# The high half of the transposed activations: a second activation from PSUM on ACT in place of a cast on DVE

## What is computed

```
h   = rmsnorm(x, g_norm1)   * (1 + sc1) + sh1          # 512 x 1024
hc  = rmsnorm(ctx, g_norm1) * (1 + mods_c1) + mods_c0  # 256 x 1024
P   = h @ w_in ; pc = hc @ w_in[:, :1312]              # split among three token mixers and the gates
x   = x + gt1 * (merge of the three mixers) @ w_out
h2  = rmsnorm(x, g_norm2) * (1 + sc2) + sh2            # 512 x 1024
x   = x + gt2 * ((silu(a) * b) @ w_ffn_out),  a, b = split(h2 @ w_ffn_in)
out = rmsnorm(x, g_final)
```

## Time and profile before

| | |
|---|---|
| median of three runs | 1573.95 us (1573.01 to 1574.51) |
| the profiled execution | 1574.66 us, of which 1572.8 us is the span from its first to its last instruction |
| PE busy | 1279.3 us, 81% of the span |
| DVE busy | 644.2 us, 41% |
| ACT busy | 369.8 us, 24% |
| POOL busy | 355.7 us, 23% |
| mean granted clock of PE | 0.864 of full speed |

### The profile page before, as it was taken

The page is one execution under the profiler, slowest core; times in us unless marked ns, Lnnn a source line. Parts: engine busy times, 40 slices in busy tenths (PEclk is TensorE's granted clock), DMA queues, the critical chain, the costliest instruction groups (busy, mean ns, idle before and its releaser), DMA issues.

```text
span 1572.8 us, 14451 instructions
## 1 busy us (share of the span) xinstructions
PE 1279.3 (81%) x5761; PEld 944.0 (60%) x5761; DVE 644.2 (41%) x1007; ACT 369.8 (24%) x458; POOL 355.7 (23%) x148
## 2 busy tenths in 40 slices
PE   5579998476966778787669787898967999999994
PEld 1246877355744556665555434665946888888883
DVE  3445225234274766766731858333432000310023
ACT  2364212031212222222104000021042222123212
POOL 2002124002021202102104011030313454455541
PEclk9988989555788887878759898999968999999998
DMA  9320224611011202112114021335351332333211
GB/s 331 106 94 27 81 78 117 103 54 54 27 59 62 60 7 74 34 37 83 35 19 175 25 82 40 113 101 187 100 142 54 88 100 94 104 84 108 83 65 54
DMA packets 137712, 131.45 MB, mean 84 GB/s; under 512 B 12986, under 2 KB 125818, under 8 KB 136621
## 3 DMA queue, kind: packets, MB, share of 16 engines
q1 hardware_dynamic: 115936, 99.81, 20.9%
q10 hardware_dynamic: 17292, 13.22, 3.7%
q0 software_dynamic: 4416, 17.50, 3.1%
HBM read 119.49 MB, written 8.91 MB: 82 GB/s over the span
## 4 chain that ended last, share of the span: by engine, by line
PE 51%; DVE 17%; issue 3%; ACT 2%; ACTq 1%; DMA 1%; POOL 1%; DVEq 0%; POOLq 0%
PE psum L640 43%; DVE buf L2008 2%; DVE buf L2007 2%; PE psum L856 1%; DVE buf L1851 1%; DVE buf L1849 1%; PE psum L838 1%; PE psum L847 1%; PE psum L794 1%; ACTq L1374 1%; PE psum L790 1%; DVE buf L2004 1%; DVE buf L1834 1%; DVE buf L1832 1%; DVE buf L1833 1%
## 5 line engine op out<-in xcount | busy, mean ns | idle before, releaser
L1115 POOL TENSOR_TENSOR ring_lo<-buf,ring_hi 128x2048 fp32r<-128x2048 f32 (+1 forms) x65 | 293.5, 4516 | 891.7 <-ACT ring_hi L1265 891.7
L640 PE MATMUL psum<-hT_hi,ring_hi 128*128 128x512 f32 x744 | 312.9, 421 | 16.9 <-DVE hT_lo L2074 10.0
L640 PE MATMUL psum<-hT_lo,ring_hi 128*128 128x512 f32 x744 | 298.6, 401 | 0.0
L640 PE MATMUL psum<-hT_hi,ring_lo 128*128 128x512 f32 x744 | 297.8, 400 | 0.0
L640 PE MATMUL psum<-buf,buf 128*128 128x512 f32 (+1 forms) x480 | 215.5, 604 | 61.8 <-DVEq L1534 15.6
L640 PEld LDWEIGHTS psum<-buf,buf 128*128 128x128 f32 x480 | 97.5, 206 | 166.3 <-issue 112.2
L1265 ACT ACTIVATE ring_hi<-buf 128x2048 fp32r<-128x2048 f32 (+1 forms) x65 | 121.9, 1875 | 306.8 <-PE psum L640 215.8
L640 PEld LDWEIGHTS psum<-hT_hi,ring_hi 128*128 128x128 f32 x744 | 146.4, 197 | 57.3 <-issue 10.7
L640 PEld LDWEIGHTS psum<-hT_lo,ring_hi 128*128 128x128 f32 x744 | 145.9, 196 | 35.6 <-issue 5.7
L640 PEld LDWEIGHTS psum<-hT_hi,ring_lo 128*128 128x128 f32 x744 | 145.1, 195 | 31.8
L2083 DVE TENSOR_TENSOR buf<-psum,buf 128x512 f32<-128x512 f32 x22 | 15.2, 692 | 220.8 <-PE psum L640 220.8
(11 more groups left out here) (313 smaller groups left out, 1878.1 us busy)
## 6 DMA issues: line engine op xcount, KB each, us to landing
buf<-in_w_in SPq DMA_DIRECT2D x26, 1024.0 KB, 5.1
buf<-in_w_mod SPq DMA_DIRECT2D x24, 1024.0 KB, 5.7
buf<-in_w_ffn_in SPq DMA_DIRECT2D x44, 512.0 KB, 5.1
buf<-in_w_ffn_out SPq DMA_DIRECT2D x8, 1024.0 KB, 5.0
scr_k<-buf POOLq DMA_DIRECT2D x4, 1024.0 KB, 5.4
buf<-scr_k POOLq DMA_DIRECT2D x4, 1024.0 KB, 8.3
buf<-in_w_out SPq DMA_DIRECT2D x4, 1024.0 KB, 6.8
buf<-in_w_ffn_out SPq DMA_DIRECT2D x4, 768.0 KB, 4.5
```

The lines of the kernel that those rows point to most:

```text
L640: ins = nc.tensor.matmul(o, a, b, start=start and n == 0, stop=stop and n == len(pairs) - 1)
L1115: nc.gpsimd.tensor_tensor(ring_lo[:, s * SLOT:s * SLOT + size], ring[:, s * SLOT:s * SLOT + size], ring_hi[:, h:h + size].bitcast(fp32), S ...
```

## The change

In both stages the cast on DVE is taken out, and ACT reads the PSUM bank twice: a first activation, with the same scale and bias, writes the high half straight from PSUM, rounded to fp32r on the way out; the second writes the 32-bit result as before and releases the bank. DVE only subtracts. DVE's wait is the same as before, for the release of the bank, so it comes after both activations. PE, POOL and SP have the same instructions in the same order.

```diff
 def h_T():   # ACT
     act.wait_ge(S("A1"), 1)
     for k in range(KD):
-        for v, tag, dst, N in ((1, "c", hcT, LC), (0, "x", hT, L)):
+        for v, tag, dst, hi, N in ((1, "c", hcT, hc_hi, LC), (0, "x", hT, hT_hi, L)):
             name = f"{tag}T{k}"
             o = full(act, name)
+            A(hi[:, k, :], o[:, 0:N], ACT.Identity, scale=A1[:, v, k:k + 1], bias=modc[:, k, v:v + 1])
             A(dst[:, k, :], o[:, 0:N], ACT.Identity, scale=A1[:, v, k:k + 1], bias=modc[:, k, v:v + 1])\
                 .then_inc(freed(name), 1)
...
 def h2_T():  # ACT
         o = full(act, name)
+        A(hT_hi[:, k, :], o, ACT.Identity, scale=A2[:, k:k + 1], bias=mod2[:, k, 0:1])
         A(hT[:, k, :], o, ACT.Identity, scale=A2[:, k:k + 1], bias=mod2[:, k, 0:1])\
             .then_inc(freed(name), 1)
...
 def h_T():   # DVE
             evacuated(dve, f"{tag}T{k}")
-            link(V.tensor_copy(hi[:, k, :], x[:, k, :]))
             V.tensor_tensor(lo[:, k, :], x[:, k, :], hi[:, k, :].bitcast(fp32), SUB)\
                 .then_inc(S("h_split"), 1)
...
 def h2_T():  # DVE
         evacuated(dve, f"x2T{k}")
-        link(V.tensor_copy(hT_hi[:, k, :], hT[:, k, :]))
         V.tensor_tensor(hT_lo[:, k, :], hT[:, k, :], hT_hi[:, k, :].bitcast(fp32), SUB)\
             .then_inc(S("h_split"), 1)
```

## The result

The change makes the kernel slightly slower. Over 13 runs of each, the median went from 1574.15 us (1568.63 to 1576.98) to 1577.83 us (1573.96 to 1579.61); the ratio is 1.0024, with a 95% interval of 1.0013 to 1.0034, so +2.0 to +5.4 us. That something was lost is clear; whether it is more or less than 0.2% isn't. The forecast was 1576.7 us, no change beyond 0.2%.

A forecast was written before the change was run, and what follows sets the result against it. PE was taken to wait in `hT` and `h2T` for DVE's last low half, with ACT's queue deciding after the change. +4.3 us in `hT` and -1.6 in `h2T` gave +2.7 on the median 1573.95: 1576.7 us, range 1574.2 to 1579.0.

The forecast's parts named there:

- What bounds the stages: In `hT` and `h2T`, PE idles 9.24 and 9.99 us for DVE's last low half; after the change DVE follows ACT.
- Part 1: In `hT`, 16 more ACT activations add 8.91 us to its queue; PE starts 4.24 us later, taken as +4.3 us.
- The rival without overlap: In ACT's queue in both stages, second activations cost full durations: +6.4 and -1.0, so +5.4 us, 1579.4; chance 0.26.
- Part 2: In `h2T`, 16 ACT activations and no long DVE cast let PE start 1.61 us earlier, taken as -1.6 us.
- The span between these points should be as before: Between PE's first product with `w_in` and ACT's first activation of `h2T`, no change in time was expected.
- The clock's allowance of 0.7 us: After PE's idle stretches in `hT` and `h2T`, the start at granted 0.50 may vary the time by 0.7 us either way.
- The total: Whole kernel: +4.3 - 1.6 = +2.7 us, giving 1576.7 us, just within 0.2% of no change.
- Slower by over 0.2%: Whole kernel's time: chance 0.37, from 0.06 of the forecast's own, 0.26 for no overlap, 0.05 for an eaten `h2T` gain.

## Why the prediction was right, and where it wasn't

**What bounds the stages: right.** PE waits for the last low half in both, ACT's queue sets the end of both after the change, and DVE idles in them.

**Part 1, +4.3 us: right.** The 32 activations took 17.81 us, as worked out (17.82); PE's start came 4.34 us later against 4.24, and the first product with `w_in` as well (132.45 against 127.95, less the 0.16 us by which this execution was late at the start). The pitch of the old activations held for the new ones, although they read a bank twice and write fp32r. The rival without overlap falls: the pitch stays at 0.45 and 0.66 us, while the recorded durations grow through the stage, from 0.57 to 0.74 us for 128x256 and from 0.78 to 0.97 us for 128x512. So for a queue of this kind the distance between starts is the price, and the duration misleads. The estimate from the Trainium skill (ScalarE: Activation LUTs, what it says of an ACTIVATE's cost under "What ACT_TABLE_LOAD costs"), 1.20 us for a pair, doesn't hold here: it is 1.12 us before and after.

**Part 2, -1.6 us: right in kind, somewhat small.** It was 2.2 us. The term that was off is the pitch: 0.70 us was taken from ACT's eight activations of before, of which the first three start 0.80 and 0.83 us apart (1174.26, 1175.06 and 1175.89). There ACT waited for PE: the transposes of the second and third bank ended at 1175.02 and 1175.86. The prediction's 0.46 us for the four transposes of a bank is a mean over `hT`; here the first banks took 0.85 us each. A second reading of the same bank hides such a wait. The sixteen took 10.63 us, 0.66 us each, the pitch that `hT` shows. The named cause, POOL's subtraction beside the last cast, is shown by the kernel in which the subtraction comes later. This trace agrees with the exclusion of DVE and POOL that the prediction cites from the Trainium skill (SBUF — State Buffer, "Reading the diagram"): 4.72 us beside POOL, 0.42 us without.

**"The span between these points should be as before": wrong.** This is the step that failed. The sum treated all code between the stages as fixed. The stretch after the scan grew by about 2.6 us in both profiles of the changed kernel, 2.0 of them from a pause that is 0.3 us longer and from the clock that falls after it, because DVE has 16 instructions fewer ahead of it; why that count delays DVE stays open. The clock's allowance of 0.7 us was put at the two known waits, where the first FFN step took 13.4, 12.7 and 13.5 us before and 12.8 and 13.1 after, and not at a third place, where the clock had stayed at 1.00 before.

**The total.** +4.3 - 2.2 + 2.6 = +4.7 us by the profiles' terms; the medians give +3.7. The profiles of before span 1572.8, 1571.1 and 1572.4 us, those of the changed kernel 1577.2 and 1574.6, 3.8 us apart in the mean. The remaining 1 us is of the size by which the stretch before the scan varies between profiles of one kernel (165.3, 164.1 and 165.5 us from the first product with `w_in` to the first matmul of the attention states, L763). The forecast of 1576.7 us is 1.1 us below the median, inside its range, through errors in both directions: 0.6 us too little gain in part 2, 2.6 us of loss not seen, and the unexplained 1 us. That the total came out so close is in part luck; the two stages by themselves are not.

**The chances.** "Slower by over 0.2%" had 0.37, mainly for the case that activations don't overlap. The measured 0.24% lies on that side by a hair, but its interval, 0.13 to 0.34%, covers both, and what brought it there was another cause.

## What to carry to other kernels

When a small operation is moved between two engines, look at which of them ends last in that stage, and price it by the distance between starts: here ACT asked 0.45 to 0.66 us where DVE asked 0.33 to 0.45, and the best kernel of those tried divides the work so that both end at about the same time. Look for an instruction that takes ten times its usual duration before moving its neighbours; in `h2T` a wait that keeps POOL off DVE gained twice what the edit did. In a kernel whose result is judged at 0.2%, profile each version twice and compare the stretches that the edit doesn't touch: if they differ steadily, the number of instructions ahead may be part of the result, and some idle instructions tell it apart. Where the profile gives "issue" for a wait, look into the kernel for a semaphore there before calling it a wait for nothing.

## What the runs showed of the hardware

- A pause of PE of 1.7 us left the granted clock at 1.00, one of 2.0 us at the same place was followed by a lower one, 0.66 over the next 5 us in the changed kernel. It was 2.0 us in all three profiles with the whole `hT` changed and DVE unpadded, 1.7 us in the nine others. 0.3 us of pause cost 2.0 us.
- 16 one-column instructions on DVE at the start, in idle time, shortened a stretch that begins 820 us later by 2.0 us (46.7 to 44.7); 16 on ACT left it at 44.6, and the time as it was (ratio 1.0002).
- A DVE cast of 128x512 took 4.72 us beside POOL's subtraction and 0.42 us without it. In the kernel before, 23 DVE instructions took over 2 us longer than the median of their line and shape, all beside a subtraction of POOL.
- Writing fp32r from PSUM cost ACT the same as writing 32-bit words: 0.78 us each, and no more for the second reading of a bank.
